# Modulation weights in a two-layer network: column matmuls one dense slot later in five stages, and modulation tiles loaded ahead of the dense ones in three

## The chip, the cores and the metric

The kernel runs on one core of a Trainium2 chip, in float32. The metric is the device time of one execution in microseconds. The core's engines are TensorE (PE in the profile, its weight loads PEld), VectorE (DVE), ScalarE (ACT), GpSimd (POOL) and SyncE (SP), which only issues transfers here.

## The reference, cut to what matters

Three layers are applied one behind the other to x of 256 tokens by 2048 channels: a state-space layer, an attention layer, and a layer with a gated delta rule, block attention and a feed-forward part. The change touches the first two, which are modulated by a conditioning vector c:

```
c_act = silu(c)                                              # 2048 values
shift, scale, gate = split(c_act @ mod_w[layer] + mod_b[layer], 3)
h = rmsnorm(x, norm_g[layer]) * (1 + scale) + shift
out = mixer(h)                                               # several products of 256 x 2048 by 2048 x n
x = x + gate * out
...
kv_shift, kv_scale = split(c_act @ kv_mod_w + kv_mod_b, 2)   # for the shared keys and values
```

So beside the dense products (256 tokens by a 2048 x 256 tile of weights each) there are vector-matrix products with c_act, whose weights (2048 x 256 tiles too) are as large as dense ones but serve one row only.

## The kernel before

All weights go through a ring of four slots in SBUF, `ring[:, 0..3]`. A slot holds a tile of 2048 x 256 floats, 2 MB. SyncE loads the tiles in program order, one DMA per tile, each after a wait that its slot is free (`load`, line 192); a slot n of the program lies in `ring[n % 4]`. `weights_in[k]` counts landed tiles, `slot_free[k]` counts freed ones. SyncE has one order: a load whose slot isn't free holds up all loads behind it.

The program is a list of stages, ORDER: mod0, u, z, glu, out, kv, kvrow, cmp, q, zc and so on. The stages in MIXED (u, z, glu, out, kv, q) have 16 slots: 8 with dense weights (D) and 8 with modulation weights (M), in pairs, D D M M, four times. In the text a pair p is D(2p), D(2p+1), M(p), M(p).

- TensorE takes a dense slot in 2 x 16 matmuls (`dense`, line 251), into the PSUM bank of the slot's number. The profile counts each as two records, so a slot is 64 of them. ScalarE drains the bank (line 388, in stage out line 464, in glu line 984) and frees the slot and the bank.
- In u, glu, out, kv and q (TURNS) VectorE takes a pair of M slots at once (`mod_pair`, line 309): 16 steps, each multiplies 512 columns by a value of c_act and adds them up in an accumulator (lines 322 and 324), with a drain between them. Then it signals `acc_ready` (line 327) and frees both slots. There are two accumulators per stage; `acc_used` says when one may be overwritten.
- TensorE then sums the accumulator over its 128 partitions with four matmuls against `ones` (`mod_columns`, line 331, matmuls on line 339), 128 x 1 each, after a wait for `acc_ready`.
- Stages mod0 and z do their modulation on TensorE as rows (line 362) and are not touched.

TensorE calls `mod_columns` behind every second dense slot (line 264). On VectorE the sums of u, glu, kv and q stand in a loop of their own (`dve_mods`, line 343): in u behind the first norm, in kv behind the norm of the key-value input (lines 490 and 494), in q behind `dve_cmp` (line 1093). In stage out they stand inside the residual (`dve_residual`, line 502): before the residual of product k (line 516), if k is even, comes `mod_pair` k/2. Behind the residual, ScalarE squares and GpSimd sums the new x, and when the last is added TensorE makes the mean square (line 449) for the next norm. Between glu and out VectorE multiplies the gated product (line 996), for which out waits.

Of the kernel before, what the change touches and what calls it, by code (L numbers as in the profile page):

```python
# [26 lines left out]
ds = bass.ds  # L27
# [51 lines left out]
BASE = {}  # L79
for _name, _n in ORDER:  # L80
    BASE[_name] = sum(n for _, n in ORDER[:len(BASE)])
COUNT = dict(ORDER)

MIXED = ("u", "z", "glu", "out", "kv", "q")

DENSE = {n: 0 if n == "mod0" else c // 2 if n in MIXED else c for n, c in ORDER}
PBASE = {n: sum(DENSE[m] for m, _ in ORDER[:k]) for k, (n, _) in enumerate(ORDER)}

PAIRS = {"mod0": 0} | {n: 8 + 4 * k for k, n in enumerate(MIXED)}

ROWS = ("mod0", "z")

TURNS = {n: 4 * k for k, n in enumerate(m for m in MIXED if m not in ROWS)}


def build(nc, t):
    ctx = ExitStack()
    with ctx:
# [29 lines left out]
        aux = ctx.enter_context(nc.psum_tensor("aux", [P, 2048], F32))  # L128
# [58 lines left out]
        def wait_free(eng, n, r):  # L187
            eng.wait_ge(slot_free[n % RING], r + n // RING + 1)
# [4 lines left out]
        def load(sp, n, r, src):  # L193
            dst, from_ = src
            wait_free(sp, n, r)
            sp.dma_start(dst(ring[:, n % RING, :]), from_).then_inc(weights_in[n % RING], 16)
# [7 lines left out]

        def stream_mixed(sp, name, src, mod_src):
            with sp.Fori(0, COUNT[name] // 8) as i:
                for p in range(2):
                    for k in (2 * p, 2 * p + 1):
                        n, r = place(name, i, k)
                        load(sp, n, r, src(i, k))  # L210
                    for x, (n, r) in enumerate(mod_slots(name, i, p)):
                        load(sp, n, r, mod_src(i, 2 * PAIRS[name] + 2 * p + x))

        def tiles_of(name, count=SLOT):

# [7 lines left out]
        def steps(eng, name, body, count=None):  # L223

            count = DENSE[name] if count is None else count
            if count // 4 > 1:
                with eng.Fori(0, count // 4) as i:
                    for k in range(4):
                        body(i, k)
            else:  # L230
                for k in range(count - count % 4):
                    body(0, k)
            for k in range(count - count % 4, count):
                body(0, k)

        def place(name, i, k):

            return (BASE[name] + k + k // 2 * 2, 2 * i) if name in MIXED else (BASE[name] + k, i)

        def mod_slots(name, i, k):  # L240

            return [(BASE[name] + 4 * k + 2 + x, 2 * i) for x in range(2)]

        def slot_ready(pe, name, i, k):
            n, r = place(name, i, k)

            wait_landed(pe, n, r)
            wait_free(pe, n, r)
            return n % RING

        def dense(pe, name, act, kd=KD, ready=None):


            def body(i, k):
                s = slot_ready(pe, name, i, k)
                w = ring[:, s, :].rearrange("p (j n) -> p j n", n=SLOT_COLS)
                for f in range(2):
                    for j in range(kd):
                        if ready and k == 0 and f == 0 and j % QUARTER == 0:
                            pe.wait_ge(ready[0], ready[1] + j // QUARTER + 1)  # L260
                        last = nc.tensor.matmul(bank[s][:, T * f:T * f + T], w[:, j, P * f:P * f + P], act[:, j, :],  # L261
                                                start=j == 0, stop=j == kd - 1)
                last.then_inc(products, 1)
                if name in TURNS and k % 2:
                    mod_columns(pe, name, i, k // 2)
            steps(pe, name, body)

        def dense_slot(pe, name, i, k, act, ready=None):
            s = slot_ready(pe, name, i, k)
# [39 lines left out]
        def mod_pair(dve, name, i, k):  # L309

            slots, acc = mod_slots(name, i, k), ACC[name]

            dve.wait_ge(acc_used, 2 * i + TURNS[name] + k + 1)
            for n, r in slots:
                wait_landed(dve, n, r)
            s0, s1 = (n % RING for n, _ in slots)
            for j in range(KD):
                at = slice(SLOT_COLS * j, SLOT_COLS * j + SLOT_COLS)

                w, a = ring[:, s0:s1 + 1, at], acc[:, k % 2]  # L320
                if j == 0:
                    nc.vector.tensor_scalar(a, w, c_act[:, j:j + 1], None, ALU.mult)  # L322
                else:
                    nc.vector.scalar_tensor_tensor(a, w, c_act[:, j:j + 1], a, ALU.mult, ALU.add)  # L324
                if j < KD - 1:
                    dve.drain()
            dve.drain().then_inc(acc_ready, 1)
            for s in (s0, s1):
                nc.vector.nop().then_inc(slot_free[s], 1)

        def mod_columns(pe, name, i, k):
            def column(x, f):
                at = 512 * MOD_BANK[name] + 4 * k + 2 * x + f
                return aux[:, slice(at, at + 1) if isinstance(i, int) else ds(8 * i + at, 1)]

            pe.wait_ge(acc_ready, 2 * i + TURNS[name] + k + 1)
            for x in range(2):
                for f in range(2):
                    last = nc.tensor.matmul(column(x, f), ACC[name][:, k % 2, x, P * f:P * f + P], ones[:, 0:1],
                                            start=True, stop=True)  # L340
            last.then_inc(acc_used, 1)
# [29 lines left out]
        def product_ready(act, name, i, k):  # L371
            act.wait_ge(products, 4 * i + PBASE[name] + k + 1)


            act.wait_ge(params_in, 16 * N_PARAMS)
            n, r = place(name, i, k)
            return n % RING
# [12 lines left out]
            steps(act, name, body)  # L390

        def wait_drained(eng, name):
            n = BASE[name] + COUNT[name] - (3 if name in MIXED else 1)

            eng.wait_ge(slot_free[n % RING], n // RING + 2)

# [46 lines left out]
        def pe_residual(pe, name, act):  # L443

            dense(pe, name, act)
            pe.wait_ge(sum_ready, 8 * SUMS[name])
            for n in range(1 if SQUARES[name][2] is None else 2):
                for f in range(2):
                    last = nc.tensor.matmul(A(n, 0, T), ones[:], sq_sum[n][:, T * f:T * f + T], start=f == 0, stop=f == 1)
            last.then_inc(ms_ready, 1)  # L450
# [384 lines left out]
        def pe_ssm(pe):  # L835
# [12 lines left out]
            def outputs(b):  # L848
# [18 lines left out]
                last.then_inc(y_ready, 1)  # L867

            wait_drained(pe, "u")
            inputs(0)  # L870
            for b in range(SBLOCKS):
# [118 lines left out]
        def dve_glu(dve):  # L990

            dve_z_bias(dve)
            wait_drained(dve, "glu")
            dve.wait_ge(yz_ready, 1)
            for q in range(4):
                nc.vector.tensor_tensor(B(2, 1024 * q, 1024), B(2, 1024 * q, 1024), B(1, 1024 * q, 1024),
                                        ALU.mult).then_inc(glu_ready, 1)
# [55 lines left out]
        def dve_cmp_in(dve):  # L1053

            wait_drained(dve, "kv")
            for k, src in ((0, KC), (1, VC)):
                for h in range(2):
                    pe_ = col("pe", 32 * k + 16 * h, 16)
                    last = nc.vector.tensor_tensor(cmp_in[k][h].rearrange("p (a l) -> p a l", l=16),
                                                   src.rearrange("p (a l) -> p a l", l=16), rep(pe_, 64), ALU.add)  # L1060
            last.then_inc(cmp_ready, 1)
# [1120 lines left out]
        def _(sp):  # L2182
# [4 lines left out]
            for name in ("u", "z", "glu"):  # L2187
                stream_mixed(sp, name, tiles_of(name), mod_tiles)
            sp.wait_ge(y_kept, SBLOCKS)
            sp.dma_start(xT[:], t["xT"]).then_inc(x_again, 16)  # L2190
            for name in ("out", "kv"):
                stream_mixed(sp, name, tiles_of(name), mod_tiles)
            stream(sp, "kvrow", tiles_of("kvrow"))
            stream(sp, "cmp", tiles_of("cmp"))
            stream_mixed(sp, "q", tiles_of("q"), mod_tiles)
            for name in ("zc", "zs", "o", "gdn", "za"):
                stream(sp, name, tiles_of(name))
# [21 lines left out]
        def _(pe):  # L2219
            pe_mean_square(pe, B(2))  # L2220
            pe_mod0(pe)
            dense(pe, "u", hT, ready=(h_ready, 0))
            pe_ssm(pe)
            pe.wait_ge(y_kept, SBLOCKS)
            dense(pe, "glu", u_all)
            pe.wait_ge(glu_ready, 4)
            pe_residual(pe, "out", tiles(B(2)))
# [299 lines left out]
```

## Time and profile before

| | us |
|---|---|
| median of 3 runs | 3486.75 (3484.26 to 3487.68) |
| profiled execution | 3484.84 |
| its span in the trace | 3482.7 |
| TensorE busy | 3284.2 (94%) |
| VectorE busy | 1423.2 (41%) |
| ScalarE busy | 474.7 (14%) |
| GpSimd busy | 127.1 (4%) |

Times in the trace are microseconds from the start of the span. An engine's busy time is summed over its instructions; what bounds the kernel is read from the waits, above all those of TensorE. Stages u to q, where the change lies, run from about 110 to 1048 us; z, which is not changed, takes about 240 to 447 of that.

### The profile page before, as it was taken

The page shows a single profiled execution, that of the slowest core. Times are in us where ns is not written, and L with a number is a line of the kernel's source. Part 1 is how long each engine was busy: PE and PEld are TensorE (multiplying, and loading weights), DVE is VectorE, ACT ScalarE, POOL GpSimd, SP SyncE. Part 2 cuts the span into 40 slices and gives each one's busy share as a digit, 9 for nine tenths or more (in the row PEclk, how much of TensorE's full clock was granted, in tenths as well). Part 3 has the DMA queues.
Part 4 walks back from the last instruction along what each step waited for, and adds up shares of the span by engine and source line. Part 5 has one row for each costly group of instructions (what it writes and reads, how often), then busy time and mean ns, then how long its engine had stood idle before and what let it go on. Part 6 is the DMA issues. An engine that isn't in the chain of part 4 may idle for free.

```text
span 3482.7 us, 50175 instructions
## 1 busy us (share of the span) xinstructions
PE 3284.2 (94%) x20868; PEld 2906.3 (83%) x20868; DVE 1423.2 (41%) x2155; ACT 474.7 (14%) x799; POOL 127.1 (4%) x89
## 2 busy tenths in 40 slices
PE   5899998989999999988999999999898999999999
PEld 4777787868888877777888887688787999999999
DVE  5447624354130133312265741161104555555443
ACT  2114410000000122211130002211000000000000
POOL 0003310000000000001000000000000000000000
PEclk9999999999999999998999999999999999999999
DMA  9763466656464422233335342232532444444443
GB/s 410 296 255 145 172 265 242 273 212 275 178 269 169 145 97 96 96 121 120 107 136 181 145 157 97 97 129 91 187 138 104 169 169 169 169 169 163 165 167 132
DMA packets 50897, 598.55 MB, mean 172 GB/s; under 512 B 9511, under 2 KB 12086, under 8 KB 13278
## 3 DMA queue, kind: packets, MB, share of 16 engines
q1 hardware_dynamic: 50782, 596.88, 45.3%
q8 instruction: 88, 1.44, 0.2%
q14 instruction: 27, 0.22, 0.0%
HBM read 593.70 MB, written 3.16 MB: 171 GB/s over the span
## 4 chain that ended last, share of the span: by engine, by line
PE 81%; DMA 9%; DVE 6%; ACT 1%; issue 1%; DVEq 1%; SPq 1%; ACTq 0%; POOLq 0%; POOL 0%
PE bank L261 27%; PE bank L2020 23%; PE bank L284 13%; DMA ring<-in_t_mod 9%; PE bank L275 5%; PE bank L296 3%; DVE E L324 3%; PE bank L2034 1%; PE aux L1209 1%; PE bank L362 1%; PE aux L1164 1%; DVE arena L324 1%; PE aux L844 0%; PE aux L1198 0%; PE bank L862 0%
## 5 line engine op out<-in xcount | busy, mean ns | idle before, releaser
L261 PE MATMUL bank<-arena,ring 128*128 128x256 f32 x3072 | 685.3, 387 | 25.6 <-DVE arena L1938 10.0
L261 PEld LDWEIGHTS bank<-arena,ring 128*128 128x128 f32 x3072 | 595.6, 194 | 112.7 <-issue 28.3
L261 PE MATMUL bank<-hT,ring 128*128 128x256 f32 x2560 | 565.1, 384 | 4.2 <-DVE hT L608 4.2
L261 PEld LDWEIGHTS bank<-hT,ring 128*128 128x128 f32 x2560 | 492.8, 193 | 73.8 <-issue 5.4
L284 PE MATMUL bank<-hT,ring 128*128 128x256 f32 x2304 | 533.7, 384 | 0.0
L284 PEld LDWEIGHTS bank<-hT,ring 128*128 128x128 f32 x2304 | 430.7, 191 | 75.4 <-issue 20.6
L2020 PE MATMUL bank<-arena,ring 128*128 128x128 f32 x3440 | 396.4, 275 | 0.0
L2020 PEld LDWEIGHTS bank<-arena,ring 128*128 128x128 f32 x3440 | 390.2, 192 | 0.0
L2020 PE MATMUL bank<-hT,ring 128*128 128x128 f32 x1680 | 197.9, 275 | 0.0
L2020 PEld LDWEIGHTS bank<-hT,ring 128*128 128x128 f32 x1680 | 192.7, 192 | 0.1
L324 DVE SCALAR_TENSOR_TENSOR E<-ring,c_act,E 128x512 f32<-128x512 f32 x240 | 180.9, 754 | 18.5 <-issue 0.6
L275 PE MATMUL bank<-hT,ring 128*128 128x256 f32 x768 | 173.0, 388 | 8.9 <-DVE hT L497 8.9
L275 PEld LDWEIGHTS bank<-hT,ring 128*128 128x128 f32 x768 | 149.4, 195 | 32.1 <-issue 11.0
L388 ACT ACTIVATE arena<-bank 128x512 f32 (+1 forms) x64 | 38.2, 597 | 719.6 <-PE bank L261 719.6
L2020 PE MATMUL bank<-arena,E 128*128 128x128 f32 x1024 | 119.7, 275 | 0.0
L1229 DVE TENSOR_TENSOR arena<-aux,con 128x60 f32<-128x60 f32 (+2 forms) x24 | 17.1, 712 | 245.6 <-PE aux L1164 245.6
L2020 PEld LDWEIGHTS bank<-arena,E 128*128 128x128 f32 x1024 | 117.0, 192 | 0.0
L322 DVE TENSOR_SCALAR E<-ring,c_act 128x512 f32<-128x512 f32 x16 | 7.8, 486 | 262.5 <-DMA ring<-in_t_mod 262.1
L2118 DVE TENSOR_TENSOR arena<-bank,w_gate 128x256 f32<-128x256 f32 x50 | 21.2, 424 | 205.9 <-ACT rstd L2063 132.8
L1636 DVE TENSOR_TENSOR W<-E,arena 128x128 f32<-128x128 f32 (+7 forms) x64 | 74.8, 1169 | 29.4 <-issue 27.8
L362 PE MATMUL bank<-ring,c_act 128*32 128x256 f32 x768 | 55.2, 436 | 30.7 <-DMA ring<-in_t_mod 30.7
L2020 PE MATMUL bank<-arena,W 128*128 128x128 f32 x688 | 82.2, 275 | 0.0
(385 smaller groups left out, 2893.8 us busy)
## 6 DMA issues: line engine op xcount, KB each, us to landing
ring<-in_t_mod SPq DMA_DIRECT2D x64, 2048.0 KB, 15.7
ring<-in_t_gu SPq DMA_DIRECT2D x44, 2048.0 KB, 7.9
ring<-in_t_out SPq DMA_DIRECT2D x16, 2048.0 KB, 7.8
ring<-in_t_zs SPq DMA_DIRECT2D x16, 2048.0 KB, 8.0
ring<-in_t_down SPq DMA_DIRECT2D x16, 2048.0 KB, 7.2
ring<-in_t_gdn SPq DMA_DIRECT2D x12, 2048.0 KB, 7.9
ring<-in_t_u SPq DMA_DIRECT2D x8, 2048.0 KB, 8.5
ring<-in_t_z SPq DMA_DIRECT2D x8, 2048.0 KB, 8.3
```

The costliest lines, as they stand in the source:

```text
L261: last = nc.tensor.matmul(bank[s][:, T * f:T * f + T], w[:, j, P * f:P * f + P], act[:, j, :], start=j == 0, stop=j == kd - 1)
L275: last = nc.tensor.matmul(bank[s][:, T * f:T * f + T], w[:, j, P * f:P * f + P], act[:, j, :], start=j == 0, stop=j == KD - 1)
L284: last = nc.tensor.matmul(bank[s][:, T * f:T * f + T], w[:, j, P * f:P * f + P], act[:, j, :], start=j == 0, stop=j == KD - 1)
L296: last = nc.tensor.matmul(bank[s][:, T * f:T * f + T], act[:, j, P * f:P * f + P], w[:, j, :], start=j == 0, stop=j == KD - 1)
L324: nc.vector.scalar_tensor_tensor(a, w, c_act[:, j:j + 1], a, ALU.mult, ALU.add)
L362: last = nc.tensor.matmul(out[32 * q:32 * q + 32, :], c_act[:, j:j + 1].to_broadcast([P, 32]), w[:, j, :], start=a == 0, stop=a == KD // 4 ...
L388: nc.scalar.activation(dst[:, at, :], bank[s][:].rearrange("p (f n) -> p f n", f=2), func, scale=scale).then_inc(slot_free[s], 1)
L1164: last = nc.tensor.matmul(aux[:, nk * h:nk * h + nk], qg[:, h, P * f:P * f + P], keys, start=True, stop=True)
L1209: last = nc.tensor.matmul(A(2), vg[:, b, kt, :], PT[:, 512 * kt:512 * kt + 512], start=kt == 0, stop=kt == f)
L1636: v.tensor_tensor(tmp, Tsol[:, :, 0:J], row, ALU.mult)
L2020: last = nc.tensor.matmul(out[:, P * q:P * q + P], a[:, j, :], b[:, j, :], start=begins and q == 0 and j == 0, stop=ends and q == len(grou ...
L2034: last = nc.tensor.matmul(bank[2 * n][:, T * f:T * f + T], w[:, j, P * f:P * f + P], hT[:, j, :], start=j == 0, stop=j == KD - 1)
```

## The change

In u, glu, out, kv and q TensorE's column matmuls for a pair are issued one dense slot later, behind the first dense slot of the next pair; the last pair's stand behind its own. TensorE's code of these stages is written out instead of looped. In out, kv and q (MODS_FIRST) the order of a pair in the ring and in SyncE's program becomes M M D D, so that M tiles lie in the slots where D tiles lay and the other way round. VectorE's, ScalarE's and GpSimd's instructions keep their order.

```diff
+MODS_FIRST = ("out", "kv", "q")
...
         def stream_mixed(sp, name, src, mod_src):
             with sp.Fori(0, COUNT[name] // 8) as i:
+                def rows(p):
+                    for x, (n, r) in enumerate(mod_slots(name, i, p)):
+                        load(sp, n, r, mod_src(i, 2 * PAIRS[name] + 2 * p + x))
+
                 for p in range(2):
+                    if name in MODS_FIRST:
+                        rows(p)
                     for k in (2 * p, 2 * p + 1):
                         n, r = place(name, i, k)
                         load(sp, n, r, src(i, k))
-                    for x, (n, r) in enumerate(mod_slots(name, i, p)):
-                        load(sp, n, r, mod_src(i, 2 * PAIRS[name] + 2 * p + x))
+                    if name not in MODS_FIRST:
+                        rows(p)
...
         def place(name, i, k):
-            return (BASE[name] + k + k // 2 * 2, 2 * i) if name in MIXED else (BASE[name] + k, i)
+            late = 2 if name in MODS_FIRST else 0
+            return (BASE[name] + k + k // 2 * 2 + late, 2 * i) if name in MIXED else (BASE[name] + k, i)
 
         def mod_slots(name, i, k):
-            return [(BASE[name] + 4 * k + 2 + x, 2 * i) for x in range(2)]
+            late = 0 if name in MODS_FIRST else 2
+            return [(BASE[name] + 4 * k + late + x, 2 * i) for x in range(2)]
...
                 last.then_inc(products, 1)
-                if name in TURNS and k % 2:
-                    mod_columns(pe, name, i, k // 2)
-            steps(pe, name, body)
+            if name not in TURNS:
+                steps(pe, name, body)
+                return
+
+            pairs = DENSE[name] // 2
+            for m in range(DENSE[name]):
+                body(m // 4, m % 4)
+                if m % 2 == 0 and m:
+                    mod_columns(pe, name, (m // 2 - 1) // 2, (m // 2 - 1) % 2)
+            mod_columns(pe, name, (pairs - 1) // 2, (pairs - 1) % 2)
...
         def wait_drained(eng, name):
-            n = BASE[name] + COUNT[name] - (3 if name in MIXED else 1)
+            n = BASE[name] + COUNT[name] - (3 if name in MIXED and name not in MODS_FIRST else 1)
```

SyncE at the loop body of stage out, before: `in_t_out` are dense tiles, `in_t_mod` modulation tiles, and the ISA rows are the waits for a free slot of the ring.

```order
L196 ISA [waits slot_free0]
L196 DMA ring<-in_t_out 128x4096
L196 ISA [waits slot_free1]
L196 DMA ring<-in_t_out 128x4096
L196 ISA [waits slot_free2]
L196 DMA ring<-in_t_mod 128x4096
L196 ISA [waits slot_free3]
L196 DMA ring<-in_t_mod 128x4096
```

The same place now:

```order
L198 ISA [waits slot_free0]
L198 DMA ring<-in_t_mod 128x4096
L198 ISA [waits slot_free1]
L198 DMA ring<-in_t_mod 128x4096
L198 ISA [waits slot_free2]
L198 DMA ring<-in_t_out 128x4096
L198 ISA [waits slot_free3]
L198 DMA ring<-in_t_out 128x4096
```

The dense loads of a pair now stand behind the modulation loads of the same pair, and these wait for the slots that VectorE frees.

TensorE at stage glu, before: a pass of the loop holds two pairs, each 64 matmuls (two dense slots) and then four column matmuls with a register row ahead of each. One pair stands here.

```order
L261 MATMUL bank<-arena,ring 128x256 x64
L336 REGISTER_ALU
L339 ISA
L339 MATMUL aux<-ones,E 128x1
L339 ISA
L339 MATMUL aux<-ones,E 128x1
```

The same stage now, complete:

```order
L271 MATMUL bank<-arena,ring 128x256 x96
L356 MATMUL aux<-ones,E 128x1 x4
L271 MATMUL bank<-arena,ring 128x256 x64
L356 MATMUL aux<-ones,E 128x1 x4
L271 MATMUL bank<-arena,ring 128x256 x64
L356 MATMUL aux<-ones,E 128x1 x4
L271 MATMUL bank<-arena,ring 128x256 x32
L356 MATMUL aux<-ones,E 128x1 x4
```

The first column matmuls moved from behind the second dense slot to behind the third, the next from behind the fourth to behind the fifth, and only the last four stayed behind the eighth.

## Rows read from the trace of the kernel before

**Rows 1.** The page's chain that ended last, shares by engine.

```profile
PE 81%; DMA 9%; DVE 6%; ACT 1%; issue 1%; DVEq 1%; SPq 1%; ACTq 0%; POOLq 0%; POOL 0%
```

**Rows 2.** Waits, whole span: us in total, times, longest us.

```profile
DVE E L322 <- DMA ring<-in_t_mod: 262.1, 15, 29.0
...
PE aux L339 <- DVEq L327: 37.2, 12, 4.6
```

**Rows 3.** Timeline, stage u: start, us, engine, instruction, [idle before <- releaser].

```profile
127.94 14.14 SPq L196 DMA_DIRECT2D ring<-in_t_u  x2
...
141.48 27.87 PE L261 MATMUL bank<-hT,ring 128*128 128x256 f32 x128
...
142.28 0.86 SPq L196 DMA_DIRECT2D ring<-in_t_mod  x2
...
160.52 0.49 DVE L322 TENSOR_SCALAR E<-ring,c_act 128x512 f32<-128x512 f32 x1 [24.29 <-DMA ring<-in_t_mod]
...
173.92 1.86 PE L339 MATMUL aux<-ones,E 128*128 128x1 f32 x8 [4.57 <-DVEq L327]
...
175.64 30.41 PE L261 MATMUL bank<-hT,ring 128*128 128x256 f32 x128
```

**Rows 4.** Timeline, the end of stage u (first row) and stage glu.

```profile
237.95 1.10 PE L339 MATMUL aux<-ones,E 128*128 128x1 f32 x8 [3.38 <-DVEq L327]
...
445.07 0.33 SPq L196 DMA_DIRECT2D ring<-in_t_glu  x1
...
462.85 0.49 DVE L322 TENSOR_SCALAR E<-ring,c_act 128x512 f32<-128x512 f32 x1 [15.80 <-DMA ring<-in_t_mod]
...
475.91 1.05 PE L339 MATMUL aux<-ones,E 128*128 128x1 f32 x8 [0.18 <-DVEq L327]
...
507.56 1.06 PE L339 MATMUL aux<-ones,E 128*128 128x1 f32 x8 [2.86 <-DVEq L327]
...
508.53 29.52 PE L261 MATMUL bank<-arena,ring 128*128 128x256 f32 x128
...
570.05 1.86 PE L339 MATMUL aux<-ones,E 128*128 128x1 f32 x8 [3.48 <-DVEq L327]
```

**Rows 5.** The page's DMA issues: KB each, median us from issue to landing.

```profile
ring<-in_t_gdn SPq DMA_DIRECT2D x12, 2048.0 KB, 7.9
```

**Rows 6.** The chain in order of time, a later stage: start, us, what.

```profile
2399.51 110.52 PE bank L261 x512
```

**Rows 7.** Timeline, stage out.

```profile
577.49 30.87 PE L261 MATMUL bank<-arena,ring 128*128 128x256 f32 x128 [5.58 <-DVE arena L996]
...
609.70 0.88 DVE L516 SCALAR_TENSOR_TENSOR xT<-arena,mod,xT  x2 [9.94 <-ACT arena L464]
...
711.48 1.34 DVE L516 SCALAR_TENSOR_TENSOR xT<-arena,mod,xT  x2 [1.60 <-ACT arena L464]
...
715.17 2.08 PE L449 MATMUL aux<-W,ones 128*128 128x256 f32 x4 [5.59 <-POOLq L437]
```

**Rows 8.** Timeline, stage kv.

```profile
722.55 30.40 PE L261 MATMUL bank<-arena,ring 128*128 128x256 f32 x128 [5.30 <-DVE arena L494]
...
730.63 0.49 DVE L322 TENSOR_SCALAR E<-ring,c_act 128x512 f32<-128x512 f32 x1 [0.44 <-issue]
...
850.07 57.04 PE L296 MATMUL bank<-ring,arena 128*128 128x256 f32 x256
```

**Rows 9.** Timeline, the end of cmp and stage q.

```profile
914.80 7.47 SPq L196 DMA_DIRECT2D ring<-in_t_mod  x2
...
923.12 27.89 PE L261 MATMUL bank<-hT,ring 128*128 128x256 f32 x128
923.22 0.68 DVE L1093 TENSOR_TENSOR W<-aux,cmp_b2r 15x512 f32<-15x512 f32 x1 [57.45 <-PE aux L1076]
...
1047.57 13.69 PE L1100 MATMUL aux<-w_gate,hT 128*128 128x48 f32 x64
```

More of the change, by code:

```diff
@@ L333, in column @@
                 at = 512 * MOD_BANK[name] + 4 * k + 2 * x + f
-                return aux[:, slice(at, at + 1) if isinstance(i, int) else ds(8 * i + at, 1)]
+                return aux[:, slice(8 * i + at, 8 * i + at + 1) if isinstance(i, int) else ds(8 * i + at, 1)]
             pe.wait_ge(acc_ready, 2 * i + TURNS[name] + k + 1)
```

## The prediction

> **What bounds the kernel now.** I read the page's chain of waits first: 81% of the chain that ended last is TensorE work, 9% is loads of modulation weights and 6% is VectorE [rows 1]. So time comes off only where TensorE waits, or where it runs slowly after a wait. The waits in total name one place that the diff touches: TensorE stands 37.2 us, in 12 waits, before the matmuls with `ones` on line 339, for VectorE's sum (released at line 327) [rows 2]. VectorE itself waits 262.1 us at line 322 for modulation weights, so it is late because its loads are late, not because it has too much to do.
>
> The timeline of stage u shows why [rows 3]. The second dense load of a pair is issued at 142.08 (the row that begins at 127.94 covers two issues and lasts 14.14), the two modulation loads right behind it at 142.28, and VectorE starts at 160.52. Its sum is there at 173.92, 13.4 us later (I use 13.3). The two dense slots began at 141.48 and took 27.87, so TensorE stands 4.57 us. The next two slots take 30.41 instead of 27.87: each wait also costs about 2.5 us of slower matmuls afterwards. In glu the same thing is 2.86 us and 29.52 [rows 4].
>
> **Figures used below.** Dense slots follow each other at 13.8 us (110.52 for 512 matmuls, which are 8 slots, in [rows 6]), a pair is 27.6. Column matmuls take 1.0 (507.56 to 508.53 in [rows 4]). Three loads in a row take 17.8 us from the first issue to use of the last (445.07 to 462.85 in [rows 4]); stage u gives 18.8 (142.08 minus the 0.33 of the issue, to 160.52). One load takes 7.9 [rows 5], so I put two at 12.9. After a wait of 3 us or more the next pair loses 1.7 to 2.5; I take 2.3.
>
> **The change, part one: the sum is asked for one dense slot later.** In u, glu, out, kv and q the columns of pair p now stand behind the first dense slot of pair p+1; only the last pair's columns stand directly behind its own slots. A slot is 13.8 us and the longest of the 12 waits is 4.6, so no wait for a sum inside a stage is left. In u and glu the load order stays, so the last pair's wait stays too, and comes earlier.
> - u: 4.57 of wait, 2.5 of slow matmuls, 0.9 of slow column matmuls (1.86 for 1.0): 7.9 us. The next pair's first dense tile is loaded behind the modulation tiles that land at 160.5; with 4.9 for one more load (17.8 less 12.9) it is there at 165.4, and the pair begins at 169.35 (173.92 less 4.57): 4 us to spare.
> - glu: 2.86 plus 1.65 (29.52 for 27.87) plus the small first wait of 0.2: 4.7 us. Its last wait of 3.48 stays, as does u's of 3.38.
>
> That is 12.6 us, and it depends on nothing but the trace.
>
> **Part two: out, kv and q load modulation first.** This takes away their last waits, since the last sum is finished before the last dense slot. The rest of the 37.2, 22.8 us (37.2 less 4.57, 3.38, 0.18, 2.86 and 3.48), is in these stages. But SP waits in order. Before, the dense loads of the next pair waited only for ScalarE's drain. Now the first of them stands behind two modulation loads, and these wait until VectorE has finished the previous sum. So wherever VectorE starts its sum late, TensorE will starve for dense weights. That must be worked out per stage, S being the start of a pair on TensorE.
>
> - *Start of out.* Its first dense tile now goes into slot 2, which glu's last sum frees, and behind a modulation load that goes into the slot of glu's last dense product. Glu's last dense slot ends at 566.57 (570.05 less 3.48). Plus 1.2 for the drain, plus 12.9 for two loads gives 580.7; before, out began at 577.49 [rows 7]. Loss 3.0 us (0 if the loads overlap well, 5 if three loads count).
> - *Inside out.* VectorE sums pair p only after the residual of the last product. Pair 0 lasts 30.6 (30.87 with a hang-over of 0.2; also slow after the wait of stage start). In the rows, slot 2 of the pair ends near 608.2, the residual begins at 609.70 and takes 0.88, so the sum starts at S+2.5. It ends at S+15.8, and three loads later, at S+33.6, the first dense tile of pair 2 is there. TensorE wanted it at S+28.6. Wait: 5.0 us, and 2.3 afterwards. Pair 1's tile is in time, since sum 0 starts before S. Pair 3's tile is too: sum 2 starts from the end of the slots, so it has the 5.0 as a lead, and 2.3 us are left over.
> - *Length of out.* 30.6 + 28.6 + 5.0 + 30.9 + 28.6, then 5.2 to the matmul of the mean square at line 449 (1.5 to the last residual, then 711.48 to 715.17 [rows 7]): 128.9 us. Before: 577.49 to 715.17, 137.7. Gain 8.8, of which some 4 us come from the last residual, which no longer queues behind a modulation sum on VectorE.
> - *kv.* VectorE makes the normalized input first and starts sum 0 at S+8.1 (722.55 to 730.63 [rows 8]). Its end is S+21.4, the first dense tile of pair 1 lands at S+39.2, wanted at S+30.2. Wait: 9.0 us, the largest new one. After that sum 1 ends 8.4 us into pair 1, and the next tile has 4.7 us to spare. Length 39.2 + 30.9 + 28.6 + 28.6 + 1.0 = 128.3; before 722.55 to 850.07, 127.5. Loss 0.8, but the row-wise product behind it starts without a wait: 57.04 becomes 55.3, gain 1.8.
> - *q.* The first dense tile waits for the first slot of cmp: issue at 914.80, use at 923.12, 8.3 us for a load of 7.9, so it just fits [rows 9]. VectorE starts sum 0 when line 1093 is done, at S+0.8. The tile of pair 1 lands at S+31.9 and is wanted at S+27.6: wait 4.4 with the rounding. Length 32.0 + 30.9 + 28.6 + 28.6 + 1.0 = 121.1; before 923.12 to 1047.57, 124.5. Gain 3.4.
>
> **The sum.** 7.9 + 4.7 - 3.0 + 8.8 - 0.8 + 1.8 + 3.4 = 22.8 us. Behind q nothing changes: the stage zc gets its slots no later than before, and what follows goes by the same tables. The profiled execution took 3484.84 (span 3482.7); 3484.8 less 22.8 is 3462.0. The median of the runs is 1.9 above that execution, so I say 3463.
>
> TensorE's code is now written out instead of looped. I cost that at nothing: the row-wise product is written out for 256 matmuls and goes at the speed of the loops, 57.04 with the slow start taken off (the cover is the queue of matmuls already issued; a visible gap of a microsecond at each of 5 stages would cost 5 us). Column matmuls lose their register work, worth a few tenths each at most.
>
> The rows give 6.3 MB in 17.8 us, 353 GB/s, for three loads. The Trainium skill (DMA: Bandwidth & Descriptors, Where 436 GB/s comes from) puts the ceiling of the ports at 435 GB/s. By it three loads could take 14.5 us, the three new waits would be 3.3 us shorter each, and the sum about 33 instead of 23; the measured 17.8 includes the start of the transfer and decides.
>
> **Rivals.**
> - *A, the sum above (0.74):* 3452 to 3472. The bounds are: three loads at 18.8 instead of 17.8 (3 us more), start of out 0 to 5 (3 less, 2 more), slow matmuls 1.7 to 2.5 per wait, and loads that come up to 3 us sooner than the row (9 less).
> - *B, the starving doesn't show (0.08):* modulation loads are issued early enough that all dense tiles are in time. Against it: the sum's start in kv is bound to the normalized input. It would give 5.0 + 9.0 + 4.4 + 3 x 2.3 = 25 us more: 3438.
> - *C, the wait only changes its name (0.10):* the round change in every stage keeps its wait, now for dense weights. One more wait of 5 and 2.3 in each of two or three places eats the gain of part two and more: 3463 + 3 x 7.3 = 3485. For it: out's pair 3 has only 2.3 us to spare.
> - *D, slower (0.08):* SP's order starves TensorE at every later pair of out, kv and q, six places more, each 7.3 us: 3463 + 44 = 3507. It decides from about four such places. Against it: once TensorE has waited, VectorE's sum has a lead and the next tile has 2.3 to 4.8 us to spare; it would need three loads to take 21 us or more.
>
> The measurement tells apart about 0.2%, 7 us. Faster by more than that: A and B, 0.82. Within: C, 0.10. Slower: D, 0.08. The predicted time is A's; the range of 8 in 10 reaches a good part of the way to B and C: 3446 to 3477.
>
> **What the changed profile would show.** No wait of TensorE before the column matmuls except two, at the ends of u and glu, near 4 us each. New waits of the dense matmuls for a load: near 5 us before the fifth slot of out, near 9 before the third of kv, near 4 before the third of q, and about 3 at the start of out. Pairs in u and glu at 28.6 all through. Stage out from its first matmul to line 449's matmul in 129 us, kv in 128, q in 121. I am wrong if waits for loads show at other pairs, or if out or kv is longer than before by over 3 us.

## The result, and the profile after

The changed kernel takes 3457.28 us (median of 4 runs, 3454.89 to 3459.87), the kernel before 3486.51 in the same series: ratio 0.9915, 95% interval 0.9904 to 0.9927. The profiled execution took 3459.03, 25.8 us less than that of before; its span is 3457.1. The prediction was 3463, with 3446 to 3477 as the range.

The six longest waits of TensorE, from stage glu to the end of q (line 271 is now the dense matmul, line 356 the column matmul, 344 the end of VectorE's sum): us in total, times, longest.

```profile
PE bank L271 <- DMA ring<-in_t_kv: 9.1, 1, 9.1
PE bank L271 <- issue: 8.0, 1, 8.0
PE bank L271 <- DMA ring<-in_t_out: 6.4, 1, 6.4
PE bank L271 <- DVE arena L511: 5.3, 1, 5.3
PE aux L356 <- DVEq L344: 4.6, 1, 4.6
PE bank L271 <- DMA ring<-in_t_q: 3.8, 1, 3.8
```

Before the column matmuls one wait of 4.6 is left in this stretch (glu's last) and one of 3.84 in u; before there were 12 with 37.2 us [rows 2]. In their place stand three waits of dense matmuls for a load, one each in kv, out and q, where the prediction had put them (9.0, 5.0 and 4.4). The 8.0 that the profile puts down to issue is the start of out, and stands below.

Timeline of the changed kernel, stage u and then kv, TensorE: start, us, instruction, [idle before <- releaser].

```profile
182.91 0.95 PE L356 MATMUL aux<-ones,E 128*128 128x1 f32 x8
183.72 27.87 PE L271 MATMUL bank<-hT,ring 128*128 128x256 f32 x128
211.44 0.95 PE L356 MATMUL aux<-ones,E 128*128 128x1 f32 x8
212.25 14.06 PE L271 MATMUL bank<-hT,ring 128*128 128x256 f32 x64
230.15 1.81 PE L356 MATMUL aux<-ones,E 128*128 128x1 f32 x8 [3.84 <-DVEq L344]
```

```profile
703.52 30.40 PE L271 MATMUL bank<-arena,ring 128*128 128x256 f32 x128 [5.30 <-DVE arena L511]
...
711.59 0.49 DVE L339 TENSOR_SCALAR E<-ring,c_act 128x512 f32<-128x512 f32 x1 [0.44 <-issue]
...
724.80 0.86 SPq L198 DMA_DIRECT2D ring<-in_t_mod  x2
725.85 9.31 SPq L198 DMA_DIRECT2D ring<-in_t_kv  x2
...
742.98 17.07 PE L271 MATMUL bank<-arena,ring 128*128 128x256 f32 x64 [9.05 <-DMA ring<-in_t_kv]
```

In u the pairs now follow each other at 28.5 us without a gap; the 30.41 of [rows 3] is gone. In kv the reader sees the price of SyncE's order. VectorE starts sum 0 at 711.59, 8.07 after TensorE, and needs 13.2. Only then, at 724.80, can SyncE issue the modulation loads, and the dense load behind them at 725.85, though its slot was free at about 721 (ScalarE drained product 0 at 720.26). It serves at 742.98, 18.2 us after the first of the three issues. The slot that waited then takes 17.07 for 14.06: another 3 us.

The stages, each from its first dense matmul to the next mark (the column matmuls at the end of glu, line 449's matmul for out), from the timelines:

| stretch | before | after | gain | predicted |
|---|---|---|---|---|
| u | 129.35 | 122.01 | 7.3 | 7.9 |
| z | 208.42 | 207.97 | 0.5 | 0 |
| glu | 122.20 | 118.08 | 4.1 | 4.7 |
| from glu's columns to out | 7.44 | 9.90 | -2.5 | -3.0 |
| out | 137.68 | 127.85 | 9.8 | 8.8 |
| kv | 127.52 | 128.92 | -1.4 | -0.8 |
| kvrow | 56.88 | 55.34 | 1.5 | 1.8 |
| cmp | 16.17 | 17.24 | -1.1 | 0 |
| q | 124.45 | 120.15 | 4.3 | 3.4 |
| gates, behind q | 13.49 | 10.22 | 3.3 | 0 |

The start of u lies 0.25 later; less that, the gains come to 25.7, and behind the gates nothing moves: from there to the end of the span it is 2421.6 us before and 2421.7 after.

How far one such row can be trusted is seen from two traces of one kernel. Against the second trace of the kernel before (`before_again`, below) the same stretches give 30.1 us, with glu at 6.0 instead of 4.1 and q at 5.2 instead of 4.3. And in three of the eleven traces of this document (`first_only`, `late_sum_mid`, `late_between`) the stretch behind the gates, which no edit touches, takes 2416.9 to 2417.2 us, in the other eight 2420.7 to 2422.3. So a stage's gain is known to 1 or 2 us, and between two profiled executions 4 or 5 us can come from a stretch that is the same in both.

### The profile page after: what moved, and what is told of

Its sections match the earlier page's. It is cut to its first block, busy times and chain, and to the rows that moved or that the text cites. A ratio compares the mean times of both kernels' runs of the same rounds, so it can differ in the third digit from the quotient of the medians.

```text
span 3457.1 us, 50025 instructions
## 1 busy us (share of the span) xinstructions
PE 3270.6 (95%) x20868; PEld 2894.0 (84%) x20868; DVE 1424.6 (41%) x2155; ACT 474.7 (14%) x799; POOL 127.6 (4%) x89
## 4 chain that ended last, share of the span: by engine, by line
PE 84%; DMA 8%; DVE 5%; ACT 1%; DVEq 1%; issue 1%; SPq 0%; ACTq 0%; POOLq 0%; POOL 0%
PE bank L271 29%; PE bank L2037 23%; PE bank L301 13%; DMA ring<-in_t_mod 6%; PE bank L292 5%; PE bank L313 3%; DVE E L341 3%; PE bank L379 1%; PE bank L2051 1%; PE aux L1226 1%; PE aux L1181 1%; DMA ring<-in_t_out 0%; DMA ring<-in_t_kv 0%; DMA ring<-in_t_q 0%; PE aux L861 0%
## 5 line engine op out<-in xcount | busy, mean ns | idle before, releaser
L2037 PE MATMUL bank<-arena,E 128*128 128x128 f32 x1024 | 119.7, 275 | 0.0
L533 DVE SCALAR_TENSOR_TENSOR xT<-arena,mod,xT x32 | 14.1, 482 | 174.3 <-ACT arena L481 173.0
```

The source lines that it names most:

```text
L2037: last = nc.tensor.matmul(out[:, P * q:P * q + P], a[:, j, :], b[:, j, :], start=begins and q == 0 and j == 0, stop=ends and q == len(grou ...
```

## The experiments

The theory T that I tested: a sum was late because its modulation loads stood in SyncE's order behind a dense load that waits for the last product's slot; and a dense load starves where it stands behind modulation loads that wait for VectorE. Both are matters of SyncE's order, so an order that avoids both should give more than the change. Rivals: modulation first is itself the gain of out, kv and q (R1); part of the gain comes from the written-out code (R2); the new waits are bandwidth (R3).

**Late columns alone** (`late_only`).

```diff
-MODS_FIRST = ("out", "kv", "q")
+MODS_FIRST = ()
```

> Only the columns come one dense slot later in all five stages; the loads keep the order D D M M everywhere. Theory T (a dense load starves only where it stands behind modulation loads that wait for VectorE): u and glu gain as in the changed kernel, 7.3 and 4.1 us; in out, kv and q the waits inside the stages go (with the slow matmuls after them 11.4, 7.2 and 6.6 us) and no dense matmul waits for a load; the last wait of each stage stays, up to 1 us longer. Sum 34 us: 3452, so faster than the changed kernel by about 5. Rival R1 (loading modulation first is where out, kv and q gain): those stages keep their length within 3 us, 3470 or more.

3463.88 us, ratio 0.9936 (0.9923 to 0.9949). T's number was missed by 12 us, on the side of the rival. By stages T holds in four of the five and fails in out. u 122.2 and glu 118.4 are as in the changed kernel; kv takes 120.6 instead of 127.5 and q 120.3 instead of 124.5, without a wait for a load. Modulation first makes kv 8.4 us longer than this. The last waits grew by more than T's 1 us in glu (3.48 to 4.98), q (3.27 to 4.50) and out (2.96 to 6.69). And out takes 137.5, as before the change, with waits for dense loads that T excluded:

```profile
639.17 0.95 PE L356 MATMUL aux<-ones,E 128*128 128x1 f32 x8
...
641.22 29.58 PE L271 MATMUL bank<-arena,ring 128*128 128x256 f32 x128 [1.10 <-DMA ring<-in_t_out]
670.64 0.95 PE L356 MATMUL aux<-ones,E 128*128 128x1 f32 x8
675.61 16.14 PE L271 MATMUL bank<-arena,ring 128*128 128x256 f32 x64 [4.02 <-DMA ring<-in_t_out]
...
698.44 1.86 PE L356 MATMUL aux<-ones,E 128*128 128x1 f32 x8 [6.69 <-DVEq L344]
```

The next rows of the same kernel, ScalarE and VectorE in out, gave a theory for it. VectorE's residual of product 2 (line 533) stands behind the sum and comes at 630.38. ScalarE's square (line 484) waits 19.84 us for it, and the drain of product 3 (line 481), which frees a slot, stands behind that square:

```profile
616.78 0.49 DVE L339 TENSOR_SCALAR E<-ring,c_act 128x512 f32<-128x512 f32 x1 [17.56 <-DMA ring<-in_t_mod]
617.36 12.35 DVE L341 SCALAR_TENSOR_TENSOR E<-ring,c_act,E 128x512 f32<-128x512 f32 x15
630.38 0.88 DVE L533 SCALAR_TENSOR_TENSOR xT<-arena,mod,xT  x2 [0.67 <-issue]
631.43 0.63 ACT L484 ACTIVATE arena<-xT  x1 [19.84 <-DVEq L535]
631.97 0.62 ACT L481 ACTIVATE arena<-bank 128x512 f32 x1
```

Product 3 ended near 625.3 (its slot began at 611.46 and takes 13.8); its drain ends at 632.6, 6 us later than it could, and the load that waits for the slot is as late. The next pair goes the same way: the drain of product 5 comes at 666.21, and the wait of 4.02 follows.

**The sum of out moved by one residual** (`late_sum_mid`), to test this theory, T2: the kernel of `late_only` with one line of `dve_residual` changed.

```diff
-                if name in TURNS and k % 2 == 0:
+                if name in TURNS and k % 2:
                     mod_pair(dve, name, i, k // 2)
```

> Late columns alone (loads D D M M), and in stage out VectorE's sum of a pair stands ahead of the residual of the second dense product instead of the first. T2 (in out, with late columns alone, dense loads come late because ScalarE waits: its square of product 2p waits for a residual that stands behind the sum, so the drain of product 2p+1, and with it the free slot and the load, comes 4 us late or more): the two waits of dense matmuls for loads in out (1.1 and 4.0 us) go and out takes 128 to 131 us instead of 137.5; the kernel 3455 to 3458. Rival (the loads of out are late for bandwidth or for the modulation loads in between): the waits stay and out takes 135 or more.

3445.94 us, ratio 0.9885 (0.9869 to 0.9902). Both load waits are gone and out takes 122.6. TensorE's waits from 560 to 700 us:

```profile
PE aux L356 <- DVEq L344: 8.2, 2, 4.3
PE bank L271 <- DVE arena L511: 5.3, 1, 5.3
PE bank L271 <- DVE arena L1013: 5.3, 1, 5.3
PE aux L466 <- POOLq L454: 2.1, 1, 2.1
```

T2 holds, and the gain in out, 14.9 us, is more than the 6.5 to 9.5 expected, since the last sum's wait in out fell too (6.69 to 3.91) and behind it only one residual is left. The kernel's time lies 9 us under the 3455 expected at least. By the traces, 14.8 of the 19.6 us against `late_only` come before the end of the gates, as much as out gained, and 4.8 behind them, in the stretch that varies by itself. This kernel beats the changed one with its loads still in the old order.

**Modulation first alone** (`first_only`).

```diff
-                if m % 2 == 0 and m:
-                    mod_columns(pe, name, (m // 2 - 1) // 2, (m // 2 - 1) % 2)
-            mod_columns(pe, name, (pairs - 1) // 2, (pairs - 1) % 2)
+                if m % 2:
+                    mod_columns(pe, name, m // 4, m // 2 % 2)
```

> Only the load order M M D D in out, kv and q; the columns stand behind their own pair again in all stages. T: with modulation first the sum of a pair is over before its second dense slot ends (S+15.8 in out, S+21.4 in kv's first pair, of 27.6), so late columns add nothing there; out, kv and q and the two products behind them gain the 14 us they gain in the changed kernel, u and glu nothing: 3472. Rival: late columns are what removes the waits there too, and the starving costs more without them: 3480 or more, with waits of 3 us or more before the column matmuls in out, kv or q.

3473.25 us (3464.71 to 3480.33), ratio 0.9962 (0.9947 to 0.9977); the scatter is wide and the median says little between the two numbers. The profile says more. TensorE's six longest waits from 560 to 1045 us:

```profile
PE bank L271 <- DMA ring<-in_t_kv: 9.1, 1, 9.1
PE bank L271 <- issue: 8.0, 1, 8.0
PE bank L271 <- DMA ring<-in_t_out: 5.6, 1, 5.6
PE bank L271 <- DVE arena L510: 5.3, 1, 5.3
PE aux L355 <- DVEq L343: 4.9, 1, 4.9
PE bank L271 <- DMA ring<-in_t_q: 3.6, 2, 3.3
```

The one wait before column matmuls is glu's last, at 576. In out, kv and q (128.6, 127.8, 119.1) there is none, and their lengths are within 1.2 us of those of the changed kernel. Where modulation is loaded first, late columns do nothing in these three stages. So R1 holds for out, where late columns alone gave nothing; in kv modulation first alone gives nothing, and in q either part alone gives about what both give.

**Written-out code alone** (`unrolled_only`): the edit of `first_only` with `MODS_FIRST = ()`, so the code of before, written out on TensorE.

> TensorE's code written out as in the changed kernel, column matmuls without registers, nothing else changed. T: no difference, 3484 to 3487. Rival R2 (part of the gain is the loop's branches and register work): 3480 or less, with shorter stages at the same waits.

3489.19 us, ratio 1.0013 (1.0004 to 1.0022). R2 falls: no gain, if anything a loss of 0.1%, 2 us over what T allowed. The loads take longer than in the first trace of before: in glu VectorE starts at 464.96, 19.5 us after the dense issue at 445.45, where [rows 4] has 17.8.

**The kernel before once more** (`before_again`), for that reason.

> The kernel before once more, for its trace. In the first trace of it a 2 MB load took 7.9 us in stages that no edit touches (gdn, gu); in the changed kernel and in the four runs so far 8.4 to 8.5. H1: that is a matter of the chip or the hour: 8.4 to 8.5 here too. H2: it belongs to the kernels with written-out code: 7.9 here, and then it is what makes the kernel with written-out code alone 0.13% slower.

3486.28 us, ratio 1.0 (0.9991 to 1.0009). The pages' rows for gdn, in the order `before_again`, the kernel with written-out code alone:

```profile
ring<-in_t_gdn SPq DMA_DIRECT2D x12, 2048.0 KB, 8.2
```

```profile
ring<-in_t_gdn SPq DMA_DIRECT2D x12, 2048.0 KB, 8.5
```

Neither hypothesis is clean. The same kernel gave 7.9 and 8.2 in two traces, so a load varies by 0.3 us by itself. All kernels with written-out code gave 8.4 or 8.5 for this row, and those with loops 7.9 to 8.2 (8.1 in `order_only`, below). Three loads in a row, issued together, took 17.5 to 18.8 us in the two traces of before, from first issue to VectorE's start, and 18.1 to 19.9 in the traces with written-out code. Instruction loading is 99 packets with written-out code and 88 with loops. Whether the code makes loads slower, or something that goes with it, stays open; between the medians of this kernel and the one with written-out code alone lie 3 us.

**SyncE's order D, M, M, D on the changed kernel** (`after_between`).

```diff
                 for p in range(2):
-                    if name in MODS_FIRST:
-                        rows(p)
                     for k in (2 * p, 2 * p + 1):
                         n, r = place(name, i, k)
                         load(sp, n, r, src(i, k))
-                    if name not in MODS_FIRST:
+                        if name in TURNS and k == 2 * p:
+                            rows(p)
+                    if name not in TURNS:
                         rows(p)
```

> The changed kernel with SyncE's order in u, glu, out, kv and q made D, M, M, D: the first dense load of a pair stands ahead of the pair's modulation loads, the slots stay as in the changed kernel. T: the waits for dense loads inside out, kv and q (6.4, 9.1 and 3.8 us) go, with 1.5 to 3 us of slow matmuls behind each, and the last waits of u and glu shrink to 2 us or less: 25 to 32 us less than the changed kernel, 3425 to 3432. Rival R3 (the waits are a matter of bandwidth: as many bytes must come in the same time, whatever the order): the waits keep two thirds of their length or more, 3450 or more.

3422.89 us, ratio 0.9813 (0.9801 to 0.9826). That is 2 us under the range expected. The waits inside out and kv are gone, those of q are 0.8 in all, and the last waits of u and glu too; one of 2.8 in glu for a dense load is new. The same bytes come in 351.3 us for out, kv and q (119.7, 116.6, 115.0) instead of 376.9, so R3 falls.

**The same order on the kernel before** (`order_only`), with loops, columns behind their own pair and slots D D M M.

```diff
                 for p in range(2):
                     for k in (2 * p, 2 * p + 1):
                         n, r = place(name, i, k)
                         load(sp, n, r, src(i, k))
-                    for x, (n, r) in enumerate(mod_slots(name, i, p)):
-                        load(sp, n, r, mod_src(i, 2 * PAIRS[name] + 2 * p + x))
+                        if k == 2 * p + (name not in TURNS):
+                            for x, (n, r) in enumerate(mod_slots(name, i, p)):
+                                load(sp, n, r, mod_src(i, 2 * PAIRS[name] + 2 * p + x))
```

> The kernel before, with one edit: in u, glu, out, kv and q SyncE loads a pair as D, M, M, D instead of D, D, M, M. Slots, columns and loops stay. T (what makes the sum late is that the modulation loads stand behind the pair's second dense load, which waits for the slot of the last dense product; 14 us earlier in the queue they are landed when VectorE is free): every sum is there before its own pair ends (at S+15.8 in out, S+21.4 in kv's first pair, of 27.6), so late columns are not needed: 3420 to 3428, no wait before the column matmuls over 1 us. Rival (the later place of the columns is needed too, for its 13.8 us of slack): 3440 or more, with waits before the columns left in at least two stages.

3420.41 us, ratio 0.9813 (0.98 to 0.9827): 66 us less than before, by the order of loads alone, more than twice what the change brings. TensorE's seven longest waits from 100 to 1055 us; there is none before the column matmuls (line 340 here):

```profile
PE bank L363 <- DMA ring<-in_t_mod: 11.8, 4, 3.8
PE bank L262 <- DVE arena L997: 5.6, 1, 5.6
PE bank L262 <- DVE arena L495: 5.3, 1, 5.3
PE bank L262 <- DVE hT L609: 4.2, 1, 4.2
PE aux L450 <- POOLq L438: 3.5, 1, 3.5
PE aux L845 <- DVE xT L920: 3.1, 1, 3.1
PE bank L262 <- DMA ring<-in_t_glu: 1.8, 1, 1.8
```

The row at line 363 is stage z and the first modulation, neither touched by the edit. Stage out shows how the order works: VectorE starts a sum 4 us after its pair begins on TensorE (587); in the kernel before it starts 19 us into the same pair (628.41 and 609.01).

```profile
586.95 27.87 PE L262 MATMUL bank<-arena,ring 128*128 128x256 f32 x128
587.53 14.77 SPq L196 DMA_DIRECT2D ring<-in_t_out  x2
...
591.37 0.49 DVE L323 TENSOR_SCALAR E<-ring,c_act 128x512 f32<-128x512 f32 x1 [2.85 <-DMA ring<-in_t_mod]
...
614.66 0.95 PE L340 MATMUL aux<-ones,E 128*128 128x1 f32 x8
```

**Late columns, old slots, order D, M, M, D** (`late_between`): `late_only` with the edit of `after_between`.

> Late columns, the slots of the kernel before (D D M M), SyncE's order D, M, M, D. T: the slots' layout does not matter, only the order of loads: same as the kernel with that order and the changed layout, 3423, within 4 us. Rival: the layout M M D D has a part in the gain: 3430 or more.

3420.82 us, ratio 0.9812 (0.9798 to 0.9825). The layout of the slots makes no difference that these medians show (3422.89 with the other layout), and late columns bring nothing that the order has not brought.

**Modulation first in out alone** (`late_first_out`), with late columns everywhere.

```diff
-MODS_FIRST = ("out", "kv", "q")
+MODS_FIRST = ("out",)
```

> Late columns in all five stages, modulation first (M M D D) in out alone. T: out as in the changed kernel (128 us against 137.5 with D D M M), kv 120.6 and q 120.3 as with D D M M, the products behind them slow-started (57.0 and 13.7): 3452 to 3457, some 3 us under the changed kernel, so modulation first pays in out only. Rival: its gain in out depends on what follows: out over 131.

One run, 3457.97 us; its span is 3456.2, 0.9 under that of the changed kernel. out takes 127.9, kv 120.5, q 120.0, kvrow 57.0, the gates 13.7, each as expected. Modulation first pays in out; in kv it costs 8.4 us and gives 1.7 back in kvrow; in q it gives nothing in the stage and 3.4 in the gates behind it. The time is 1 us over the range expected; a single run, it tells no difference from the changed kernel.

## Why the prediction was right

*Which waits go.* Shown. The waits for sums inside the stages are gone, with the slow pairs behind them; u and glu keep their last one (3.84 and 4.62; expected near 4). Their gains came out 0.6 short each. The last waits, which I had kept at their old size, were 0.5 and 1.1 longer. In glu the delay can be followed back: sum 1 began 19.8 us after the first issue of its three loads (469.45 to 489.21), where the same three took 17.6 before; from then on each pair of modulation loads waited for the slots that the last sum freed, and the last sum began at 545.44, 15.4 us after its two loads were issued (530.03). All this is smaller than what glu differs by in the two traces of the kernel before (122.20 and 124.05).

*The three new waits.* Shown, place by place: 6.4, 9.1 and 3.8 against 5.0, 9.0 and 4.4. That they come from the order is shown by the order D, M, M, D, which takes them away with the same bytes. For out, 0.8 of the 1.4 us too little lie in the sum, whose slots were free for SyncE 14.1 us after its start (600.37 to 614.44) instead of 13.3, and 0.5 in its three loads, which took 18.3 us (614.44 to 632.73) instead of 17.8.

```profile
600.37 0.48 DVE L339 TENSOR_SCALAR E<-ring,c_act 128x512 f32<-128x512 f32 x1 [0.36 <-issue]
600.95 13.18 DVE L341 SCALAR_TENSOR_TENSOR E<-ring,c_act,E 128x512 f32<-128x512 f32 x15
...
614.44 0.86 SPq L198 DMA_DIRECT2D ring<-in_t_mod  x2
...
615.49 12.07 SPq L198 DMA_DIRECT2D ring<-in_t_out  x2
...
632.73 15.89 PE L271 MATMUL bank<-arena,ring 128*128 128x256 f32 x64 [6.43 <-DMA ring<-in_t_out]
```

By the ports' ceiling of 435 GB/s that I had weighed from the Trainium skill (DMA: Bandwidth & Descriptors, Where 436 GB/s comes from) three loads could take 14.5 us. They took 17.5 to 19.9 us in these traces, from first issue to first use, 316 to 360 GB/s. The ceiling itself fits the traces: in the middle of such a group the kernel before moved 433 GB/s (148 to 157 us). So the 3 us and more over 14.5 lie at the start and the end of the group. The same section of the Trainium skill says that for transfers between HBM and SBUF the HBM side, at about 358 GB/s, is what binds. The trace, with 433, does not agree.

*Out's length.* 127.85 against 128.9. Its first three slots took 43.1 us (568.29 to 611.43), 1.7 over three times 13.8, where I had carried 3.0 over from before; that and a shorter end outweigh the longer wait in the middle. That the last residual no longer queues behind a sum holds: from the last column matmuls to the mean square there are 4.5 us (691.68 to 696.14) instead of 6.6 (708.53 to 715.17), and the mean square's own wait is 3.51 instead of 5.59 [rows 7]. Counted from the end of the last dense slot to the mean square it is 4.5 us instead of 9.6, so 5.1 less, where I had said some 4.

*Start of out, kv, kvrow, q.* Within 1 us each. (My figures for the start of out give 3.2, 580.7 less 577.49, where I wrote 3.0.) The wait at out's start is 8.04 instead of 5.58; it disappears (5.3, for VectorE) in `late_only` and in `after_between`. `late_only` has glu's last sum as late and the old slots, so the slots are needed. That the late sum is needed too, as the step had it, is not shown by itself: `after_between` takes it away together with the order of the loads.

*What the sum lacked.* The gates behind q: 3.3 us, the largest term that I had at zero. I had assumed that slow matmuls follow a wait only in dense stages. In the kernel before the 64 narrow matmuls of the gates ran slow nearly from beginning to end, in the changed one only in part; the windows of before and of after (PEclk, the third number from the end, is the granted clock, here 0.53 and 0.70):

```profile
1047.00:1061.00 14.00, 14.00 (x71) 14.00 (x71) 0.17 (x1) 0.00 (x0) 0.00 (x0) 0.53 0.98 419
```

```profile
1025.00:1035.00 10.00, 10.00 (x66) 10.00 (x66) 0.17 (x1) 1.54 (x2) 0.00 (x0) 0.70 0.57 211
```

The 0.53 is almost all of the time at 1.2 GHz; ahead of it TensorE had waited 3.27 us. In the changed kernel there is no wait ahead, and the clock is at 2.4 GHz for the first 4 us of the gates (1.00 up to 1028, 0.50 from 1029 on). The loads are not the reason, though the DMA share in the two windows differs too (0.98 and 0.57): in `after_between` the gates take 10.1 us at a DMA share of 1.02 and 433 GB/s.

Against this stands cmp, 1.1 us longer: its last matmuls ran at a granted clock of 0.58 (902.2 to 905.0) instead of 1.00. The second trace of the kernel before has the same slow matmuls (1.75 us for line 1076, 1.05 in the first), so that is no effect of the change. Without the gates the errors cancel to 0.2 us, which is luck in part; with them the profiled execution gained 25.8 where 22.8 were forecast. The median gained 29.2, because two of the four runs lie 4 us under the profiled one; why, no trace shows.

*The written-out code.* I had cost it at nothing. Alone it measures 1.0013: a few us against the change, not found by stage.

*What I did not see.* The sum was right and the frame too narrow. I took the late sum as given and asked what moving its consumer brings; the load that made it late could be moved instead, at no cost, for 66 us. And for `late_only` I missed the chain through ScalarE in out: sum, residual, square, drain, slot, load. The trace of the kernel before has it too: there the drain of product 3 comes at 643.59, 6 us after it could. No dense matmul waited for a load there, so I did not look at it.

## What to carry to other kernels

When a consumer waits for a producer that is idle most of the time, look at what the producer waits for, before moving the consumer: here its loads stood in one in-order queue behind a load that waited for something else. In such a queue, put each load where its slot is free first; check for each kind of load what the one ahead of it waits for. And when an engine's drain frees the slots, nothing that waits for another engine's long work should stand ahead of the drain.

## What the runs showed of the hardware that I had not expected

Narrow matmuls lost the clock while they ran, and did not get it back. The gates' 64 matmuls of 48 columns took 13.5 to 13.7 us behind a wait of 3.1 to 4.5 us (six traces, granted clock 0.50 to 0.53), and 9.2 to 10.3 us without one (five traces, 0.69 to 0.77). Without a wait they started at 1.00 and fell to 0.50 some 4 to 5 us in, with TensorE busy throughout; the clock came back only within the dense matmuls behind them (at 1039 in the changed kernel, 4 us into these). Matmuls of 60 columns kept 1.00 for all of their 14.4 us (887.8 to 902.2 in the changed kernel).

The same thing is behind most of the 4 or 5 us by which the untouched stretch varies: 64 matmuls of 16 columns, behind dense ones and without a wait, took 11.2 us in eight traces and 8.3 in the three short ones. In the kernel before the clock had fallen 3 us into them, in `late_sum_mid` 6 us into them.

Dense matmuls of 256 columns lost 1.5 to 3 us behind a wait of 3 to 9 us (15.53 and 17.07 for 14.06) and were back at full speed within the pair. The time of the same 2 MB load varied between traces of the same kernel by 0.3 us (7.9 and 8.2).
